# Interleaving a chunk's square with its high part, and an earlier row-sum matmul, at the two GLU feed-forwards of a two-block transformer kernel

## What is computed

```python
for layer in (0, 1):                                    # block 2
    h = rms_norm_2(x, ln_mix_pre[layer])
    m = even_mixer(h, ...) if layer == 0 else odd_mixer(h, ...)
    x = x + rms_norm_2(m, ln_mix_post[layer])
    h = rms_norm_2(x, ln_ffn_pre[layer])                # x * rsqrt(mean(x^2) + eps) * g
    x = x + rms_norm_2(swiglu(h, w_gate, w_up, w_down), ln_ffn_post[layer])

def swiglu(h, w_gate, w_up, w_down):
    return (silu(h @ w_gate) * (h @ w_up)) @ w_down     # 1024 -> 2 x 2816 -> 1024
```

## Time and profile before

| | |
|---|---|
| Time, median of 3 runs | 3698.87 us (3696.71 to 3700.15) |
| The profiled execution | 3703.82 us |
| Its span in the trace | 3702.1 us |
| TensorE busy | 3423.9 us (92%) |
| VectorE busy | 1934.0 us (52%) |
| ScalarE busy | 1377.8 us (37%) |
| GpSimd busy | 304.0 us (8%) |

### The profile page before, as it was taken

The page is one execution under the profiler, slowest core; times in us unless marked ns, Lnnn a source line. Parts: engine busy times, 40 slices in busy tenths (PEclk is TensorE's granted clock), DMA queues, the critical chain, the costliest instruction groups (busy, mean ns, idle before and its releaser), DMA issues.

```text
span 3702.1 us, 42516 instructions
## 1 busy us (share of the span) xinstructions
PE 3423.9 (92%) x17714; PEld 2873.0 (78%) x17714; DVE 1934.0 (52%) x2766; ACT 1377.8 (37%) x2151; POOL 304.0 (8%) x238
## 2 busy tenths in 40 slices
PE   7898898999999988898899999888999888889997
PEld 6778777888888876787677888767888677768886
DVE  5574655777636545655445544635343455444343
ACT  4563443333313334534434334333222345343221
POOL 0000000221101110000011001210000210210002
PEclk9999999999999999999999999999999889999999
DMA  5101114433324321011243322221222210112222
GB/s 207 35 22 60 49 45 151 152 130 122 117 75 140 122 75 46 19 60 61 73 143 107 121 100 89 101 80 71 97 103 94 74 40 29 57 57 90 100 93 70
DMA packets 74497, 321.97 MB, mean 87 GB/s; under 512 B 8897, under 2 KB 17857, under 8 KB 52289
## 3 DMA queue, kind: packets, MB, share of 16 engines
q1 hardware_dynamic: 74304, 319.25, 25.0%
HBM read 303.49 MB, written 15.73 MB: 86 GB/s over the span
## 4 chain that ended last, share of the span: by engine, by line
PE 50%; DVE 5%; ACT 4%; issue 1%; POOL 1%; DMA 0%; POOLq 0%; SPq 0%; ACTq 0%; DVEq 0%
PE psum L658 14%; PE psum L659 14%; PE psum L660 14%; DVE split_weights L629 1%; PE psum L1166 1%; ACT split_weights L618 1%; POOL arena L2035 1%; PE psum L1178 1%; DVE arena L1456 0%; PE psum L2783 0%; PE psum L671 0%; PE psum L2759 0%; PE psum L1192 0%; PE psum L672 0%; PE psum L673 0%
## 5 line engine op out<-in xcount | busy, mean ns | idle before, releaser
L658 PE MATMUL psum<-split_inputs,split_weights 128*128 128x512 f32 (+1 forms) x2872 | 1056.3, 368 | 17.2 <-DVE split_weights L629 14.4
L659 PE MATMUL psum<-split_inputs,split_weights 128*128 128x512 f32 (+1 forms) x2872 | 1047.2, 365 | 0.0
L660 PE MATMUL psum<-split_inputs,split_weights 128*128 128x512 f32 (+1 forms) x2872 | 1046.0, 364 | 0.0
L629 DVE TENSOR_TENSOR split_weights<-arena,split_weights 128x2048 fp32r<-128x2048 f32 (+3 forms) x246 | 507.7, 2064 | 484.0 <-ACT split_weights L618 483.5
L658 PEld LDWEIGHTS psum<-split_inputs,split_weights 128*128 128x128 f32 x2872 | 545.6, 190 | 111.1 <-DVE split_weights L629 17.8
L659 PEld LDWEIGHTS psum<-split_inputs,split_weights 128*128 128x128 f32 x2872 | 545.4, 190 | 87.3 <-issue 3.2
L660 PEld LDWEIGHTS psum<-split_inputs,split_weights 128*128 128x128 f32 x2872 | 544.7, 190 | 86.3
L618 ACT ACTIVATE split_weights<-arena 128x2048 fp32r<-128x2048 f32 (+3 forms) x246 | 414.2, 1684 | 164.3 <-PE psum L660 164.1
L658 PE MATMUL psum<-split_hidden,split_weights 128*128 128x512 f32 (+1 forms) x880 | 324.1, 368 | 2.1 <-DVE split_weights L629 2.0
L659 PE MATMUL psum<-split_hidden,split_weights 128*128 128x512 f32 (+1 forms) x880 | 323.9, 368 | 0.0
L660 PE MATMUL psum<-split_hidden,split_weights 128*128 128x512 f32 (+1 forms) x880 | 323.7, 368 | 0.0
(11 more groups left out here) (335 smaller groups left out, 4927.2 us busy)
## 6 DMA issues: line engine op xcount, KB each, us to landing
arena<-w_up_dram SPq DMA_DIRECT2D x44, 1024.0 KB, 4.9
arena<-ffn_up_dram SPq DMA_DIRECT2D x44, 1024.0 KB, 4.8
arena<-w_ada_dram SPq DMA_DIRECT2D x80, 512.0 KB, 3.7
arena<-w_in_dram SPq DMA_DIRECT2D x32, 1024.0 KB, 4.8
arena<-w_down_dram SPq DMA_DIRECT2D x32, 704.0 KB, 4.1
arena<-ffn_down_dram SPq DMA_DIRECT2D x32, 704.0 KB, 4.1
arena<-od_w_in_dram SPq DMA_DIRECT2D x13, 1024.0 KB, 4.8
arena<-w_ada_dram SPq DMA_DIRECT2D x8, 1024.0 KB, 12.7
```

The costliest lines, as they stand in the source:

```text
L629: dve.e.tensor_tensor(ws[:, i, 1, 0:nk * w], raw_view(key), ws[:, i, 0, 0:nk * w].bitcast(F32), ALU.subtract).then_inc(*w_lo(*key))
L658: pe.e.matmul(dst, a[0], b[0], start=i == 0, stop=False)
L659: pe.e.matmul(dst, a[0], b[1], start=False, stop=False)
L660: ins = pe.e.matmul(dst, a[1], b[0], start=False, stop=i == n - 1)
```

## The change

Two edits, both of which apply to both feed-forwards. In `act_gained` the second loop over chunks is gone: the square of chunk c now stands right behind the high part of chunk c, where before all eight squares stood behind all eight high parts. With the squares, the six adds of GpSimd, which wait for them, can come earlier; GpSimd's own list is unchanged. In `pe_glu` the condition of `pe_square_summed` goes from weight block 1 to weight block 0: TensorE's two sum instructions stand 48 matmuls earlier. No instruction is added or removed.

```diff
@@ act_gained
             for c in range(DC):
                 act.wait_ge(halves_sum, y_site, c)
                 act.e.activation(h2_part(c, *ALL)[0], X2[:, c, :], ACT.Copy, scale=v2(l, "ffn_pre", c)).then_inc(
                     *h_hi(site, c))
-            for c in range(DC):
                 act_square_summed(site, ALL, c, DC, T2, 1, X2[:, c, :])
             act_prepare()
@@ pe_glu
-                    if (half, m) == (0, 1):
+                    if (half, m) == (0, 0):
                         pe_square_summed(site, ALL, DC, T2, 1)
```

## The result

The changed kernel takes 3708.54 us (median of 7 runs, 3705.32 to 3713.29), the kernel before beside it 3699.92 (7 runs, 3696.69 to 3701.73). The ratio is 1.0024, with a 95% interval from 1.0014 to 1.0034: 8.6 us slower. Forecast were 3703.3 and +4.4, with a range up to 3708.0.

What follows compares the result with a forecast made beforehand. TensorE, busy 92% of the span, was taken as the bound. Two feed-forwards at 4.3 us less the 4.2 won in the first gave +4.4 on the median 3698.87, so 3703.3 us; range 3695 to 3708.

Steps and rivals of the forecast that it cites:

- Part 1: ScalarE's squares between the high parts fit its idle time: nothing, at most 0.1 us per feed-forward.
- Part 2: GpSimd's six adds now meet VectorE's chain in block 0 and delay TensorE by 4.3 us per feed-forward (2.5 to 5.2).
- 0.84: Microseconds that each GpSimd add was taken to cost VectorE in block 0; ends 0.54 and 0.98.
- whole-instruction rival: Each add holds VectorE for its whole 1.295 us record: 7.1 us per feed-forward, +10.0 in all, 3708.9 us; chance 0.07.
- The 0.70 us in hand: TensorE's slack at block 0's last chunk, behind the last low part, subtracted from the adds' delay in each feed-forward.
- Part 3: TensorE's sum ahead of block 1 finds its input ready: no wait, same cost at either place.
- Part 4: Earlier norm shortens TensorE's gap before block 4, first feed-forward: 2.6 us of waiting plus 1.6 of low clock, 4.2 won.
- Side by side: Rival: the adds in block 0 cost VectorE nothing, leaving only the gain of 4.2 us: 3694.7 us; chance 0.10.
- The clock in block 0: Rival: TensorE's granted clock falls in half-idle block 0, up to 1.6 us more per feed-forward: +7.6, 3706.5 us; chance 0.13.
- The gap: Rival: the first feed-forward keeps its 2.9 us gap before block 4 and its clock loss: +8.6, 3707.5 us; chance 0.06.

Runs made afterwards that it cites:

- the half-size adds: The changed kernel with GpSimd's twelve adds on 256 of the 512 columns, the other half of the sum left out: 3702.65 us in one run.
- the memset: The changed kernel with GpSimd's twelve adds replaced by writes of zeros into the same accumulator, sum of squares left out: 3695.25 us in one run.

## Why the prediction was wrong, step by step

**Part 1, the squares (nothing): right.** With the adds out of the way block 0 ends to 0.02 us where it did.

**Part 2, the adds (4.3 us per feed-forward): the mechanism right, the term mis-sized. This is the step that failed.** It read "6 x 0.84 - 0.70 = 4.3". Measured is 6 x 1.04 - 0.1 = 6.1 (24.03 - 17.85 = 6.18 in the first, 23.98 - 17.84 = 6.14 in the second). Two numbers in it were off, and in the same direction.

The 0.84 was taken from L2035 beside L2015 because the shapes were the same. They were, but L710's own record was in the rows, 1.295 us, and L2035's shortest record is 1.084, by the source view of the kernel before:

```profile
L2035 POOL TENSOR_TENSOR arena<-arena x16: 1084/1537/1541, 2882.1 to 3693.4; 128x512 f32<-128x512 f32 x16
```

The prediction set the 0.84 beside the 1.295 of L710, though it belongs to the 1.084 of L2035. The hold should have been carried over with the length of the add: 0.84 + 0.20 = 1.04, which is what the half-size adds bear out (0.26 less than the record at either size); by proportion it would have been 0.84 x 1.29 / 1.09 = 0.99. The row that pointed there, 0.98 for the first L710 against L1524, was the same instruction at the price it has here, and was made the upper end. The trace of before thus held the number, and "the instructions have the form of those here" was the wrong test: VectorE's had, GpSimd's had not the same length. The Trainium skill (SBUF — State Buffer, "SBUF: two separate sides") gives whichever starts first the shared ports for its whole instruction. The runs show that nearly, 0.26 us less than the add's record alone: 1.03 of 1.29 us, 0.84 of 1.09 and 0.48 of 0.74. The Trainium skill (SBUF — State Buffer, "Who interferes with whom") also says that a GpSimd instruction which only writes does not contend with such a VectorE instruction; the memset agrees, with no VectorE record above 0.75 us. The whole-instruction rival's 7.1 us per feed-forward was 1.0 too high, mine 1.8 too low.

The 0.70 us in hand were read off chunk 7, since I had the sixth add hold up the low part of chunk 7. It comes one instruction earlier, on the sum L2025 of chunk 7, which stands ahead of the low part of chunk 6, and there TensorE had 0.2 in hand (of which it lost 0.1 again, since the first matmul behind a wait lasts 0.50 instead of 0.39). The order on both engines was known, and the sixth add does come as long behind the sum of chunk 6 as foretold; but VectorE is one instruction further back, because the fifth add holds it between the two (L1982 at 3324.30). The prediction had one add fall into each chunk. They come in pairs: while VectorE is held, ScalarE goes on and delivers the next square. With both numbers read so, the sum is 2 x 6.1 - 4.2 = +8.0.

**Part 3, the sum (nothing): right with the early squares.** It follows block 0 without a wait, at 3331.34. Without the early squares it costs 6.5 us of waiting and a fallen clock.

**Part 4, the gap (-4.2 us, the first feed-forward only): right.** Block 0's end came 6.18 us late and block 8's start only 2.21, so 3.97 were won. Blocks 3 and 4, whose starts were 13.79 and 12.59 us from those of the next, now take 11.36 and 11.05: 2.4 from the wait (forecast 2.6) and 1.5 from the clock (1.6). From start to start block 4 is still 11.36 - 48 x 0.227 = 0.5 us late, forecast 0.3. The kernel that only splits block 3 early wins 4.6.

**The rivals.** Side by side is false for adds, but it is what the memset shows (net -4.2, forecast -4.2). The clock in block 0 did not fall. The whole instruction is false by 0.26 us an add, yet with +10.0 it lay nearer to the result than the forecast did. The gap did not stay.

**The range.** Its upper end, +9.1 over 3698.87, was below the result by half a microsecond. The term's own upper end was 5.2; with the slack at 0 and the 0.98 of the earlier trace rows it would have been 5.9, and the whole instruction 7.8. The slack was given no range at all. As a change, +8.6 lies inside that +9.1 only because the range was widened for the rivals; the sum's own ends, +0.8 to +6.2, miss it. And the next profile was to read about 3708 and reads 3708.12, which is luck: it reached the first feed-forward 7.75 us earlier than the profile of before and lost 3.6 of these again between the two feed-forwards.

## What to carry to other kernels

Work moved to an idle engine isn't free if it reads SBUF beside VectorE's two-input instructions: price it by that very instruction's length in the trace where it runs alone, here less 0.26 us, and not by a neighbour of the same shape. When a chain is delayed step by step, the slack that counts is that of the first consumer behind the last delay, so move the chain along, hold by hold, before reading it. And look for what an earlier result releases: here the whole gain came from a weight split that stood behind the norm by its place in two lists, and moving that alone gives 0.9986 (0.9977 to 0.9995) with none of the cost.

## What the runs showed of the hardware

The time for which a GpSimd instruction holds up a VectorE instruction with two SBUF inputs of 128x512: nothing for a memset (its record 0.53 us), 0.36 to 0.41 for a copy of 128x512 (shortest record 0.75, none alone), 0.48 for an add of 128x256 (0.74 alone), 0.84 for an add of 128x512 whose operands lie far apart (1.09 alone), and 1.03 for one whose accumulator lies beside the rows (1.29 alone). For the adds that is the record alone less 0.25 to 0.26 us at all three lengths. VectorE holds GpSimd as well: an add that came while L629 ran took 2.95 us instead of 1.09. The record alone depends on where the two operands lie, by 0.20 us of 1.29, and a shift by 32 bytes leaves it; the cause wasn't found. TensorE's granted clock was 1.00 from 3316 to 3331 us, with waits of up to 1.3 us every 3 us.
